# Feed-forward down projections as seven block products in place of eight

## The chip, the cores and the metric

The kernel runs on one core of a Trainium2 chip. What counts is the device time of one execution, in microseconds (us), as the median of several runs. The engines are named as the profile names them: PE is TensorE (matrix products), PEld its weight loads, DVE is VectorE, ACT is ScalarE, POOL is GpSimd and SP is SyncE, which here only issues transfers.

## What the reference computes

A network over 256 tokens of width 1024, in float32 throughout. Its front is two layers of three sublayers; four of these six sublayers are gated feed-forward blocks:

```
def swiglu(h, w_gu, w_down):                     # h: 256 x 1024
    gate, up = jnp.split(h @ w_gu, 2, axis=-1)   # w_gu: 1024 x 5632
    return (jax.nn.silu(gate) * up) @ w_down     # w_down: 2816 x 1024

def sublayer(x, shift, scale, gate, g_pre, g_post, fn, res_weight):
    h = rmsnorm(x, g_pre) * (1 + scale[:, None, :]) + shift[:, None, :]
    return x + res_weight * gate[:, None, :] * rmsnorm(fn(h), g_post)
```

Shift, scale and gate ("modulation") of every sublayer are products of one conditioning row with a large weight matrix, 11 such matrices in all. The other two sublayers are a gated linear attention and a latent attention. The tail is a short convolution, differential attention and two expert layers, each of which gathers 128 rows of 8 KB for each of the 256 tokens from a table.

## The kernel before

**Stages.** The front is eight stages in one fixed order: ffn, gla, ffn, kv, ffn, mla, ffn, conv (numbered 0 to 7, so the feed-forward stages are 0, 2, 4 and 6). The 256 tokens are two blocks of 128, b = 0 and 1. Every engine runs its own written-out list of instructions, with counting semaphores between the lists, and each list is worked off in order.

**First part of a feed-forward stage** (`ffn` on PE, the matmuls of L975). The hidden width 2816 is 22 tiles of 128. For each tile a unit of 16 float32 matmuls of 256 columns makes gate and up in one PSUM bank (three banks `psW` in turn; a unit opens only when the unit three before has been stored). ACT takes the silu, DVE multiplies (L2207) and stores one tile of `actT` (in `arena`), and counts `unit_stored`. The profile records each float32 matmul as two rows.

**Second part** (`project`, L893). 22 tiles of activations times 22 weight tiles of 128 x 1024, for two token blocks and two halves of 512 columns: 88 matmuls of 512 columns that sum into `psF[:, b, :]`. It begins when DVE has stored the last tile. The last 12 matmuls are those of block 1 for tiles 16 to 21, so block 0 is complete 12 matmuls before the end. Then ACT makes block 0's root mean square, DVE adds it to `x` (`finish`) and scales the next stage's input (`prepare`), and PE, behind its last down matmul, transposes that input (L786) for the next stage.

**Weights.** SP loads them into `ring`, four slots of 2 MB each: 11 loads of gate and up, 6 of down (four tiles each, the last two), then the next stage's. A slot is filled again when `w_used` (down) or `unit_full` (gate and up) says that it is free.

**Modulation.** The modulation matrices come as 120 halves of 1 MB. POOL issues their loads into three buffers (`modulation_weights`, L509), each when the one three before was used; DVE multiplies and sums each in two instructions of 1024 elements (`half_step`, L2032). They are spread over the feed-forward stages by `halves_done`: 4/3 of a half for each unit of the first part, and what is left (6 of 32 in stages 0 and 6, 2 of 28 in stages 2 and 4) in the second, by a loop after the last unit. DVE has them in its list between the units' products.

**Kept chunks.** Three 1 MB chunks of tail weights (numbers 3, 6 and 9) are loaded into `arena` by SP between the conv stage's first weight loads.

## Time and profile before

| what | us |
| --- | --- |
| median of 3 runs (2773.39 to 2774.01) | 2773.78 |
| span of the profiled execution | 2775.9 |
| first part of a feed-forward stage, 640 matmul rows | 138.2 to 138.5 |
| down projection of one stage, 176 matmul rows | 75.8 |
| front, up to the first gathered rows of the tail | 1358.7 |
| tail, from there on | 1417 |

The profiled execution's span is 2.1 us above the median of the runs; its own device time is not given apart. The page cuts the span into 40 slices of 69.4 us. The GB/s row is what all transfers of the core moved in a slice. In stretches given as A:B, the figures are the length, then busy time of PE, PEld, DVE, ACT and POOL with their instructions, the granted TensorE clock, the DMA share and GB/s.

### The profile page before, as it was taken

The page shows a single profiled execution, that of the slowest core. Times are in us where ns is not written, and L with a number is a line of the kernel's source. Part 1 is how long each engine was busy: PE and PEld are TensorE (multiplying, and loading weights), DVE is VectorE, ACT ScalarE, POOL GpSimd, SP SyncE. Part 2 cuts the span into 40 slices and gives each one's busy share as a digit, 9 for nine tenths or more (in the row PEclk, how much of TensorE's full clock was granted, in tenths as well). Part 3 has the DMA queues.
Part 4 walks back from the last instruction along what each step waited for, and adds up shares of the span by engine and source line. Part 5 has one row for each costly group of instructions (what it writes and reads, how often), then busy time and mean ns, then how long its engine had stood idle before and what let it go on. Part 6 is the DMA issues. An engine that isn't in the chain of part 4 may idle for free.

```text
span 2775.9 us, 26672 instructions
## 1 busy us (share of the span) xinstructions
PE 2463.2 (89%) x9819; PEld 1566.6 (56%) x9819; DVE 1601.6 (58%) x3550; ACT 620.1 (22%) x1778; POOL 685.0 (25%) x698
## 2 busy tenths in 40 slices
PE   7999999999999999999998877967988778877776
PEld 6874558856884678758654432634535535432222
DVE  4552144524451545513697885686887877874445
ACT  2001210001000220000143333342333533332222
POOL 1110001100110001100243443444444443444332
PEclk9999999999999999999999999989999989999999
DMA  9994427954894339957799999999999999999997
GB/s 382 383 372 165 152 95 271 361 231 152 319 363 170 144 149 380 370 202 269 293 376 421 421 422 421 413 412 421 415 421 400 421 421 415 421 392 422 421 422 326
DMA packets 120520, 931.58 MB, mean 336 GB/s; under 512 B 15133, under 2 KB 16565, under 8 KB 20422
## 3 DMA queue, kind: packets, MB, share of 16 engines
q0 software_dynamic: 94032, 670.65, 59.1%
q1 hardware_dynamic: 26358, 259.23, 23.7%
q8 instruction: 77, 1.26, 0.2%
q14 instruction: 53, 0.43, 0.0%
HBM read 928.74 MB, written 1.09 MB: 335 GB/s over the span
## 4 chain that ended last, share of the span: by engine, by line
PE 58%; DMA 27%; DVE 8%; ACT 3%; issue 2%; SPq 1%; POOL 1%; DVEq 0%
DMA ring<-in_peer_uv_dram,lamt 26%; PE psR L975 20%; PE psF L893 11%; PE psF L1325 10%; DVE ring L2567 3%; PE psR L863 2%; PE psR L833 2%; PE psR L822 2%; PE psR L1350 1%; POOL ring L679 1%; PE psR L1422 1%; PE psF L921 1%; PE psR L874 1%; ACT small L1765 1%; PE psF L1192 1%
## 5 line engine op out<-in xcount | busy, mean ns | idle before, releaser
L1325 PE MATMUL psF<-ring,p_diag 128*128 128x512 f32 x1792 | 868.2, 629 | 248.0 <-ACT p_diag L1771 247.7
L679 POOL DMA_INDIRECT ring<-in_peer_uv_dram,lamt x512 | 592.8, 1158 | 984.3 <-PE psF L1325 757.9
L2567 DVE SCALAR_TENSOR_TENSOR ring<-ring,h 128x1024 f32<-128x1024 f32 x512 | 620.9, 1223 | 345.5 <-DMA ring<-in_peer_uv_dram,lamt 342.4
L1325 PEld LDWEIGHTS psF<-ring,p_diag 128*128 128x128 f32 x1792 | 337.0, 198 | 709.3 <-ACT p_diag L1771 369.4
L975 PE MATMUL psR<-hT,ring 128*128 128x256 f32 x2560 | 553.3, 379 | 0.6 <-DMA ring<-in_gu_t_dram 0.6
L975 PEld LDWEIGHTS psR<-hT,ring 128*128 128x128 f32 x2560 | 486.2, 190 | 66.5 <-DMA ring<-in_gu_t_dram 0.7
L893 PE MATMUL psF<-ring,arena 128*128 128x512 f32 x704 | 303.2, 593 | 4.0 <-DVE arena L2207 4.0
L1762 ACT ACTIVATE small<-small 128x2 f32<-128x2 f32 x255 | 51.8, 203 | 825.6 <-DVE ring L2567 825.4
L893 PEld LDWEIGHTS psF<-ring,arena 128*128 128x128 f32 x704 | 133.5, 190 | 172.0 <-issue 166.4
L509 POOL DMA_DIRECT2D mring<-in_mod_t_dram x80 | 42.5, 531 | 746.3 <-DVE mring L2032 742.2
L2207 DVE TENSOR_TENSOR arena<-arena,psR 128x256 f32<-128x256 f32 x80 | 33.7, 421 | 249.7 <-ACT arena L1632 249.6
L1771 ACT ACTIVATE p_diag<-ident,small 128x128 f32<-128x128 f32 x446 | 158.2, 395 | 8.3
L1632 ACT ACTIVATE arena<-psR 128x256 f32<-128x256 f32 x86 | 33.0, 384 | 568.7 <-PE psR L975 522.7
L1765 ACT ACTIVATE small<-small,gout 128x1 f32<-128x1 f32 x510 | 122.4, 287 | 8.3
L2032 DVE SCALAR_TENSOR_TENSOR mring<-mring,M 128x1024 f32<-128x1024 f32 x96 | 113.6, 1220 | 13.4 <-DMA mring<-in_mod_t_dram 13.3
L2122 DVE RECIPROCAL small<-small 128x1 f32<-128x1 f32 x12 | 1.9, 157 | 201.6 <-ACT small L1616 201.6
L509 POOL DMA_DIRECT2D M<-in_mod_t_dram x40 | 21.2, 530 | 331.3 <-DVE M L2032 301.9
L2549 DVE SCALAR_TENSOR_TENSOR hT<-ring,small,hT 128x1024 f32<-128x1024 f32 x62 | 79.5, 1282 | 26.9 <-ACT small L1765 26.6
L1410 PEld LDWEIGHTS psR<-hT,mring 128*128 128x128 f32 x768 | 89.2, 192 | 9.6 <-issue 9.6
L1410 PE MATMUL psR<-hT,mring 128*128 128x128 f32 x768 | 89.6, 275 | 0.0
L2009 DVE COPY arena<-psR 128x512 f32<-128x512 f32 (+5 forms) x48 | 29.9, 629 | 90.0 <-PE psR L863 53.7
L2032 DVE SCALAR_TENSOR_TENSOR mring<-mring,p_diag 128x1024 f32<-128x1024 f32 x64 | 75.7, 1220 | 10.4 <-DMA mring<-in_mod_t_dram 10.3
(341 smaller groups left out, 2289.3 us busy)
## 6 DMA issues: line engine op xcount, KB each, us to landing
ring<-in_gu_t_dram SPq DMA_DIRECT2D x44, 2048.0 KB, 9.0
mring<-in_mod_t_dram POOLq DMA_DIRECT2D x80, 1024.0 KB, 7.8
M<-in_mod_t_dram POOLq DMA_DIRECT2D x40, 1024.0 KB, 8.1
ring<-in_down_t_dram SPq DMA_DIRECT2D x20, 2048.0 KB, 9.3
mring<-in_tail_w_dram SPq DMA_DIRECT2D x40, 1024.0 KB, 9.3
ring<-in_conv_in_t_dram SPq DMA_DIRECT2D x12, 2048.0 KB, 8.1
ring<-in_gla_in_t_dram SPq DMA_DIRECT2D x6, 2048.0 KB, 7.7
ring<-in_out_t_dram SPq DMA_DIRECT2D x6, 2048.0 KB, 7.7
```

Of the source, the lines that this page charges most:

```text
L509: eng.dma_start(half_rows[i % HALVES].rearrange("p k n -> p (k n)"), w).then_inc(m_loaded[i % HALVES], 16)
L679: pool.indirect_dma_start(out=pair(n % PAIRS), out_offset=None, in_=rows, in_offset=bass.IndirectOffsetOnAxis(ap=s_idx[:, c:c + 1], axis=0 ...
L822: ins = pe.matmul(ps[:, t * P:(t + 1) * P], w[:, k, t * P:(t + 1) * P], hT[:, k, b * P:(b + 1) * P], start=(k == 0), stop=(k == KD - 1))
L893: ins = pe.matmul(psF[:, b, f * HALF:(f + 1) * HALF], lhs[:, k, b * P:(b + 1) * P], w[:, k % 4, f * HALF:(f + 1) * HALF], start=(k == 0), ...
L975: ins = pe.matmul(ps[:, part * T:(part + 1) * T], w[:, k, part * 256 + c * P:part * 256 + (c + 1) * P], hT[:, k, :], start=(k == 0), stop= ...
L1325: ins = pe.matmul(psF[:, b, f * HALF:(f + 1) * HALF], p_diag[:, n % PAIRS, :], row_v(n % PAIRS)[:, f * HALF:(f + 1) * HALF], start=(i == 0 ...
L1410: ins = pe.matmul(ps[:, t * P:(t + 1) * P], w[:, k, t * P:(t + 1) * P], hT[:, k, b * P:(b + 1) * P], start=(k == 0), stop=(k == KD - 1))
L1765: act.activation(p_w[:, c + s:c + s + 1], p_gel[:, c + s:c + s + 1], ACT.Copy, scale=s_g[:, b, i + s:i + s + 1]).then_inc(w_ready, 1)
L1771: act.activation(p_diag[:, c + s, :], ident[:], ACT.Copy, scale=p_w[:, c + s:c + s + 1])\
L2032: ins = dve.scalar_tensor_tensor(w[:, t, :], w[:, t, :], 1.0, cond_row[st.n >= 7], ALU.mult, ALU.mult, accum_out=dst[:, t:t + 1])
L2549: ins = dve.scalar_tensor_tensor(sums, row, p_w[:, c:c + 1], sums, ALU.mult, ALU.add)
L2567: dve.scalar_tensor_tensor(row_u(c), row_u(c), 1.0, h[:, b, :], ALU.mult, ALU.mult, accum_out=p_dots[:, c:c + 1]).then_inc(dot_done, 1)
```

## The change

The 22 tiles of the hidden width are taken as 11 pairs (k, kk) = (2p, 2p + 1). For each pair, with token blocks A (two tiles by two blocks) and weight halves B (two tiles by two halves of 512), the eight block products become seven, and the results are combined by adds after the sums over the pairs are complete.

- PE: `project` for down is replaced by `down`: 77 matmuls of 512 columns into seven banks. Pairs 0 to 4 run all seven products; pairs 5 to 8 run products 1, 6, 7, 5, 4; then the last two pairs run these five product by product; then come products 2 and 3 of pairs 5 to 10 (12 matmuls). It begins one unit's store earlier (`have(u - 2)`).
- POOL: `sum_weights` makes for each pair four differences of 128 x 512 in SBUF, two of them linked by a wait each. There are two buffers, in the place of `h` (even pairs) and `hT` (odd pairs). Pair 0 runs four halves before the stage's last half is issued; pair 1 waits until the first part has no unit left; pairs 2 to 10 wait until product 4 of the pair two before is done. All are ahead of the next stage's modulation loads in POOL's list.
- DVE: `sum_acts` makes four sums of 128 x 128 for each pair, between the units' products. `sum_products` and `sum_second` combine the seven banks into `psF` (eight instructions of 512 columns), and ACT waits for `down_summed` in place of the matmuls.
- Modulation: `halves_done` spreads all of a stage's halves over the units up to tile 21, 1.6 a unit in stages 0 and 6 and 1.4 in stages 2 and 4. None is left for the second part.
- Loads: the down tiles are stored in the order 0 to 9, then 10, 12, ... 20, then 11, 13, ... 21. Kept chunk 6 now comes first, and chunks 3 and 9, whose homes hold sums of activations, wait for the end of stage 6.

```diff
-PRELOADED = (3, 6, 9)
+PRELOADED = (6, 3, 9)
+PAIRED = FT // 2
+LATE_PAIRS = range(5, PAIRED)
+DOWN_ORDER = [k for p in range(5) for k in (2 * p, 2 * p + 1)] + [2 * p for p in LATE_PAIRS] + [2 * p + 1 for p in LATE_PAIRS]
+ACT_SUMS = (7552, 10752, 10752, 8704)
...
+    def act_sum(which, m, p):
+        q = m * PAIRED + p
+        return arena[:, ACT_SUMS[which] + q * P:][:, 0:P] if q < 30 else macc[:, 0, (q - 30) * P:(q - 29) * P]
+    def down_tile(st, k):
+        q = DOWN_ORDER.index(k)
+        return slot(st.w + 11 + q // 4, 4, D)[:, q % 4, :]
+    def product_bank(st, product):
+        if product in (6, 7):
+            return psW[(st.u + 17 + product) % 3]
+        return {1: psM[:], 4: psF[:, 0, 0:HALF], 5: psF[:, 0, HALF:], 2: psF[:, 1, 0:HALF], 3: psF[:, 1, HALF:]}[product]
...
-        return min(2 * len(BESIDE[st.n]), max(unit - 1, 0) * 4 // 3)
+        return min(2 * len(BESIDE[st.n]), max(unit - 1, 0) * 2 * len(BESIDE[st.n]) // 20)
...
-            if c in PRELOADED:
+            if c == PRELOADED[0]:
                 sp.wait_ge(x_ready, x_count(6))
+            elif c in PRELOADED:
+                sp.wait_ge(w_used, outputs[ffn3.w + LOADS["ffn"] - 1])
...
-                if st is conv7 and j in (2, 3, 4):
-                    load_kept(PRELOADED[j - 2])
+                if st is conv7 and j in (2, 4, 5):
+                    load_kept(PRELOADED[(2, 4, 5).index(j)])
...
+        def sum_weights(st, p):
+            k, kk = 2 * p, 2 * p + 1
+            w, ww = down_tile(st, k), down_tile(st, kk)
+            if p >= 2:
+                pool.wait_ge(weights_sums_used, (PAIRED - 2) * st.which + p - 1)
+            for i in sorted({down_slot(k), down_slot(kk)}):
+                pool.wait_ge(w_loaded[home_of(st.w + 11 + i)], landed[st.w + 11 + i])
+            if p == 1:
+                pool.wait_ge(unit_full, st.u + UNITS["ffn"])
+            if p == 0:
+                pool.wait_ge(unit_stored, st.u + 6)
+            t2, t3, t4 = [weight_sums[p % 2][:, m, :] for m in range(3)]
+            b11, b12, b21, b22 = w[:, 0:HALF], w[:, HALF:], ww[:, 0:HALF], ww[:, HALF:]
+            pool.tensor_tensor(t3, b22, b12, ALU.subtract)
+            link(pool.tensor_tensor(b12, b12, b11, ALU.subtract))
+            link(pool.tensor_tensor(t2, b22, b12, ALU.subtract))
+            pool.tensor_tensor(t4, b21, t2, ALU.subtract).then_inc(weights_summed, 1)
...
+                    for before, p in ((4, range(0, 1)), (0, range(1, PAIRED))):
+                        for st in stages:
+                            if st.kind == "ffn" and i == 2 + sum(2 * len(BESIDE[k]) for k in BESIDE if k <= st.n) - before:
+                                for q in p:
+                                    sum_weights(st, q)
+            if n == len(PIECES):
+                for p in range(1, PAIRED):
+                    sum_weights(ffn3, p)
...
-        def project(st, i, lhs, kt):
...
+        def down(st):
+            def product(m, p):
+                k, kk = 2 * p, 2 * p + 1
+                w, ww, sums = down_tile(st, k), down_tile(st, kk), weight_sums[p % 2]
+                lhs, rhs = {1: (actT[:, k, P:], w[:, 0:HALF]), 2: (actT[:, kk, P:], ww[:, 0:HALF]),
+                            3: (act_sum(st.which, 2, p), ww[:, HALF:]), 4: (actT[:, kk, 0:P], sums[:, 2, :]),
+                            5: (act_sum(st.which, 0, p), w[:, HALF:]), 6: (act_sum(st.which, 1, p), sums[:, 0, :]),
+                            7: (actT[:, k, 0:P], sums[:, 1, :])}[m]
+                return pe.matmul(product_bank(st, m), lhs, rhs, start=(p == 0), stop=(p == PAIRED - 1))
+            def sums_ready(p):
+                pe.wait_ge(act_summed, PAIRED * st.which + p + 1)
+                pe.wait_ge(weights_summed, PAIRED * st.which + p + 1)
+            for p in range(PAIRED - 2):
+                sums_ready(p)
+                for m in (1, 6, 7, 5):
+                    ins = product(m, p)
+                if p == 6:
+                    ins.then_inc(w_used, 1)
+                product(4, p).then_inc(weights_sums_used, 1)
+                if p not in LATE_PAIRS:
+                    for m in (2, 3):
+                        ins = product(m, p)
+                    if p in (1, 3):
+                        ins.then_inc(w_used, 1)
+            for m in (1, 6, 7, 5, 4):
+                for p in (PAIRED - 2, PAIRED - 1):
+                    if m == 1:
+                        sums_ready(p)
+                    ins = product(m, p)
+                    if m == 4 and p == PAIRED - 2:
+                        ins.then_inc(w_used, 1)
+                ins.then_inc(first_ready if m == 4 else product_done, 1)
+            for m in (2, 3):
+                for p in LATE_PAIRS:
+                    ins = product(m, p)
+                    if m == 3 and p == 8:
+                        ins.then_inc(w_used, 1)
+                ins.then_inc(product_done if m == 2 else w_used, 1)
...
-            have(u - 1)
-            project(st, st.w + 11, actT, FT)
+            have(u - 2)
+            down(st)
...
-                    output_done(act, st, b)
+                    if st.kind == "ffn":
+                        act.wait_ge(down_summed, TB * st.which + b + 1)
+                    else:
+                        output_done(act, st, b)
...
+                if j % 2 == 0:
+                    dve.wait_ge(unit_stored, u - 1)
+                    sum_acts(st, j // 2 - 1)
-            while halves_taken.n < sum(2 * len(BESIDE[n]) for n in BESIDE if n <= st.n):
-                half_step()
+            dve.wait_ge(unit_stored, u)
+            sum_acts(st, PAIRED - 1)
+            if st.n == 0:
+                tables()
+            sum_products(st)
+        def sum_acts(st, p):
+            k, kk = 2 * p, 2 * p + 1
+            b0, b1 = [[actT[:, t, b * P:(b + 1) * P] for t in (k, kk)] for b in range(TB)]
+            s1, s2, s4 = [act_sum(st.which, m, p) for m in range(3)]
+            link(dve.tensor_tensor(s1, b0[0], b0[1], ALU.add))
+            dve.tensor_tensor(b0[0], b1[0], b0[0], ALU.subtract)
+            link(dve.tensor_tensor(s2, s1, b1[0], ALU.subtract))
+            dve.tensor_tensor(s4, b1[1], s2, ALU.subtract).then_inc(act_summed, 1)
+        def sum_products(st):
+            done = 5 * st.which
+            dve.wait_ge(product_done, done + 1)
+            dve.tensor_copy(sum_p1, product_bank(st, 1)).then_inc(product_summed, 1)
+            dve.wait_ge(product_done, done + 2)
+            dve.wait_ge(product_summed, 4 * st.which + 1)
+            dve.tensor_tensor(sum_p16, product_bank(st, 6), sum_p1, ALU.add).then_inc(product_summed, 1)
+            dve.wait_ge(product_done, done + 3)
+            dve.wait_ge(product_summed, 4 * st.which + 2)
+            dve.tensor_tensor(sum_p167, product_bank(st, 7), sum_p16, ALU.add).then_inc(product_summed, 1)
+            dve.wait_ge(product_done, done + 4)
+            ps = product_bank(st, 5)
+            dve.tensor_tensor(sum_p165, ps, sum_p16, ALU.add).then_inc(product_summed, 1)
+            dve.wait_ge(product_summed, 4 * st.which + 4)
+            dve.tensor_tensor(ps, ps, sum_p167, ALU.add)
+            dve.wait_ge(first_ready, sum(s.kind != "kv" for s in stages[:st.n + 1]))
+            ps = product_bank(st, 4)
+            dve.tensor_tensor(ps, ps, sum_p167, ALU.add).then_inc(down_summed, 1)
+        def sum_second(st, half):
+            if half == 0:
+                dve.wait_ge(product_done, 5 * st.which + 5)
+                ps = product_bank(st, 2)
+                dve.tensor_tensor(ps, ps, sum_p1, ALU.add)
+            else:
+                output_done(dve, st, 1)
+                ps = product_bank(st, 3)
+                dve.tensor_tensor(ps, ps, sum_p165, ALU.add).then_inc(down_summed, 1)
...
-            if st.n == 0:
-                tables()
                     finish(st, b)
+                if st.kind == "ffn" and b == 0:
+                    sum_second(st, 0)
                 if b or st.kind not in ("kv", "mla"):
                     prepare(every[st.n + 1], b)
+                if st.kind == "ffn" and b == 0:
+                    sum_second(st, 1)
...
-    given["down_t"] = np.stack([tile(w) for w in inputs["ffn_w_down"].reshape(4, FF, D)])
+    given["down_t"] = np.stack([tile(w.reshape(FT, P, D)[DOWN_ORDER].reshape(FF, D)) for w in inputs["ffn_w_down"].reshape(4, FF, D)])
```

## Rows read from the trace of the kernel before

**Rows 1.** The page: its head, and granted clock and GB/s by slice

```profile
span 2775.9 us, 26672 instructions
...
PEclk9999999999999999999999999989999989999999
...
GB/s 382 383 372 165 152 95 271 361 231 152 319 363 170 144 149 380 370 202 269 293 376 421 421 422 421 413 412 421 415 421 400 421 421 415 421 392 422 421 422 326
```

**Rows 2.** Chain of waits, start to first mixer: start us, us, what

```profile
48.09 138.41 PE psR L975 x640
187.49 75.80 PE psF L893 x176
```

**Rows 3.** Stretches of the span: its us, busy time by engine, clock, DMA share, GB/s

```profile
48.00:186.50 138.50, 138.40 (x640) 121.56 (x640) 73.20 (x163) 7.30 (x19) 18.31 (x35) 1.00 0.96 385
187.00:263.30 76.30, 75.81 (x178) 33.68 (x179) 25.42 (x61) 5.93 (x10) 3.70 (x7) 1.00 0.54 209
...
1018.60:1156.80 138.20, 138.16 (x641) 121.30 (x639) 71.07 (x152) 7.67 (x21) 21.89 (x42) 1.00 0.91 353
...
1233.60:1300.00 66.40, 65.11 (x496) 57.48 (x495) 20.94 (x60) 1.40 (x3) 0.00 (x0) 1.00 0.85 339
...
1358.70:2775.00 1416.30, 1143.25 (x3935) 602.55 (x3933) 1020.46 (x2230) 479.28 (x1473) 586.93 (x507) 0.96 0.99 411
```

**Rows 4.** Groups by line and shape, whole span

```profile
L893 PE MATMUL psF<-ring,arena 128*128 128x512 f32 x704 | 303.2, 593 | 4.0 <-DVE arena L2207 4.0
...
L2516 DVE TENSOR_TENSOR macc<-gains,small 128x512 f32<-128x512 f32 x32 | 22.2, 694 | 1.1
...
L2448 DVE SCALAR_TENSOR_TENSOR arena<-arena 128x128 f32<-128x128 f32 x32 | 9.1, 346 | 0.3
```

**Rows 5.** Timeline where the down projection of stage 2 begins

```profile
570.68 0.42 DVE L2207 TENSOR_TENSOR arena<-arena,psR 128x256 f32<-128x256 f32 x1 [4.00 <-ACT arena L1632]
...
571.15 15.29 PE L893 MATMUL psF<-ring,arena 128*128 128x512 f32 x35 [1.00 <-DVE arena L2207]
...
573.68 0.53 POOL L509 DMA_DIRECT2D M<-in_mod_t_dram  x1 [6.38 <-DVE M L2032]
```

**Rows 6.** Timeline of GpSimd's own arithmetic: start us, us

```profile
5.30 0.40 POOL L709 CAST dist<-dist 128x256 f32<-128x256 int32 x1
5.85 0.40 POOL L710 TENSOR_SCALAR_AFFINE_SELECT dist<-dist 128x256 f32<-128x256 f32 x1 [0.15 <-POOL dist L709]
...
6.53 0.20 POOL L713 CAST small<-small 128x16 f32<-128x16 int32 x1
```

**Rows 7.** Stretches of the tail: two idle gaps, each with what follows

```profile
1818.30:1823.00 4.70, 0.03 (x2) 0.00 (x0) 2.29 (x7) 2.70 (x9) 1.56 (x2) 1.00 1.00 415
1823.50:1826.90 3.40, 3.40 (x7) 1.58 (x6) 3.38 (x6) 0.03 (x1) 0.09 (x1) 0.50 1.02 424
1896.80:1902.30 5.50, 0.02 (x1) 0.00 (x0) 3.64 (x7) 1.64 (x5) 2.69 (x2) 0.97 1.01 422
1902.00:1905.40 3.40, 3.08 (x4) 1.17 (x4) 3.36 (x4) 0.27 (x1) 0.00 (x0) 0.50 1.02 424
```

**Rows 8.** Timeline of VectorE near the end of stage 0's first part

```profile
173.54 1.22 DVE L2032 SCALAR_TENSOR_TENSOR mring<-mring,M 128x1024 f32<-128x1024 f32 x1
...
176.22 1.23 DVE L2032 SCALAR_TENSOR_TENSOR mring<-mring,M 128x1024 f32<-128x1024 f32 x1
```

**Rows 9.** Who waited for whom, first part of stage 0

```profile
DVE mring L2032 <- DMA mring<-in_mod_t_dram: 8.4, 4, 3.5
```

**Rows 10.** Timeline, end of stage 0's down projection

```profile
253.02 1.02 ACT L1615 ACTIVATE h<-psF 128x1024 f32<-128x1024 f32 x1 [36.97 <-PE psF L893]
...
260.36 0.75 DVE L2110 TENSOR_SCALAR h<-x,small 128x1024 f32<-128x1024 f32 x1
...
263.12 1.04 PE L786 MATMUL psR<-ident,h 128*128 128x128 f32 x8
...
263.84 2.65 DVE L2086 TENSOR_SCALAR hT<-psR,small 128x128 f32<-128x128 f32 x8 [2.72 <-PE psR L786]
```

More of the change, by code:

```diff
@@ L314, in _program @@
     m_reduced = sem("m_reduced")
+    act_summed = sem("act_summed")
+    weights_summed = sem("weights_summed")
+    weights_sums_used = sem("weights_sums_used")
+    product_done = sem("product_done")
+    product_summed = sem("product_summed")
+    down_summed = sem("down_summed")
     unit_full = sem("unit_full")
```

27 lines of the change are left out of this document (6 added, 21 removed).

## The prediction

> **What bounds the kernel now.** I read the slices of the page first. From slice 21 to the end the transfers run at 400 to 422 GB/s in nearly every slice [rows 1]; that is the tail, and as one stretch it is at a DMA share of 0.99 [rows 3]. The change touches nothing in it, so the tail should only move as a block: what the front gains or loses is the result. In the front I read the chain of waits. The first feed-forward stage stands in it with two long pieces and nothing beside them: 138.41 us of gate and up matmuls, then 75.80 us of down matmuls [rows 2]. Stages 2, 4 and 6 repeat them within 0.3 us. So PE sets the time there, and a PE microsecond saved or lost in a feed-forward stage counts in full, four times over. The stretches show what lies beside it: in the first part of stage 0, PE is busy 138.40 of 138.50 us and the transfers are at a share of 0.96, 385 GB/s; in the second part DVE, ACT and POOL are nearly free and the transfers at 209 GB/s [rows 3]. The granted clock is 1.00, the 2.4 GHz level, in these stretches.
>
> **The terms on PE.** One float32 matmul of 512 columns takes 75.80 / 88 = 0.861 us (two recorded rows each) [rows 2, 4]. Eleven fewer are 9.5 us. The second part also begins sooner: at its start PE waits 1.00 us for DVE's product of the last tile [rows 5], 4.0 us over the four stages [rows 4]; `have(u - 2)` asks for the tile before, long stored. Together 10.5 us a stage, 42 us in all. That is the most the change can give.
>
> **What GpSimd takes back.** The sums of weights are new on POOL, and PE waits for them at the head of each pair. No two-input arithmetic of GpSimd is in this trace. Its one-input operations take 0.40 us for 256 columns and 0.20 us for 16 [rows 6], so 0.20 + 0.20 x 496/240 = 0.61 us for 512. Lower bound of a two-input difference of 512 columns: the same 0.61 us. Upper bound: two such passes, 1.22 us. I take 1.2 us, near the upper end, because this engine's rows grow with each element that it reads, and the second operand is a second reading. A linked operation starts 0.15 us after the one before [rows 6]; with two links a pair costs G = 4 x 1.2 + 0.3 = 5.1 us. By the bounds G is 2.7 to 5.2 us.
>
> The Trainium skill's page "GPSIMD Engine Reference", section "Performance versus the Vector engine", gives 4497 ns for a `tensor_tensor` add of 2048 float32 columns, about twice VectorE's, and advises against such work on GpSimd. A quarter of it is 1.12 us, an estimate from that page: G would be 4.8 us and the change some 5 us better than my sum. No run here shows it yet.
>
> Now the schedule, from PE's start of the part at 0. Pairs 0 to 4 take 7 x 0.861 = 6.03 us each, pairs 5 to 10 have only five products ahead, 4.31 us each. Pair 0's sums are made during the first part. Pair 1's need `hT`, free at 0, and are there at 0.2 + 5.1 = 5.3, before 6.03: no wait, with 0.7 us in hand. Pairs 2 to 6 have room. From then on PE's step is 4.31 us and POOL's is 5.1. POOL can start pair 7 when product 4 of pair 5 is done, at 5 x 6.03 + 4.31 = 34.5, and wakes 0.2 to 0.3 us later (POOL's issue at 573.68 after DVE's work that ended at 573.4) [rows 5]. It then makes pairs 7, 8, 9 and 10 without pause, so pair 10 is ready at 34.7 + 4 x 5.1 + 0.1 = 55.2. PE would want it at 30.15 + 4 x 4.31 + 0.86 = 48.2, because the last two pairs run product by product and pair 10 is wanted after a single matmul of pair 9. PE loses 7.0 us: about 1.1 + 0.8 + 0.8 at pairs 7 to 9 and 4.3 at pair 10. Even fast sums leave a part: POOL may start pair 10 only when PE starts pair 9, so the wait is at least G + 0.3 - 0.86, 2.1 us at G = 2.7.
>
> **What the clock takes back.** In the tail PE idled for 4.70 and 5.50 us in two stretches at 1.00 and 0.97, and in the 3.4 us that followed the granted clock was 0.50, the 1.2 GHz level, in both [rows 7]. The 4.3 us before pair 10 is such a gap. At half clock 3.4 us do the work of 1.7: I add 1.7 us a stage. Bounds: 0 if the clock stays, 3.4 if the low level lasts twice as long.
>
> **DVE and the boundary.** Combining costs eight instructions of 512 columns, 0.69 us each by the nearest row [rows 4]. Six lie under PE's last products; on block 0's way lies one, after product 4. Before, block 0's input for the next stage was ready at 260.36 + 0.75 = 261.1, and PE came to it at 263.12 [rows 10]: 2.0 us in hand, and the add takes 0.8. `sum_second(0)` falls into DVE's wait for ACT's root. `sum_second(1)` stands ahead of the storing of the transposed input: it starts when PE ends, about 263.3, takes 0.69, and the storing starts near 264.05, in place of 263.84. I count 0.2 us a stage. ACT's square of block 1 comes 0.7 us later, but its root then waited for DVE anyway. If the 2.0 us in hand were gone, the add would cost 0.8 us a stage.
>
> **The first part.** Sums of activations: 44 instructions of 128 columns a stage, 0.35 us each by the nearest row [rows 4], 1.4 us in every second unit. A half of modulation takes 2.7 us of DVE (173.54 to 176.22) [rows 8]. In stage 0 a unit then asks of DVE 1.6 x 2.7 + 0.42 + 0.7 = 5.4 us of its 6.9. It fits, and PE meets a late DVE only when it is about two units (13.8 us) behind, or one unit at the start of the second part. The transfers are the tighter side: 385 GB/s for 138.5 us are 53.3 MB; some three more halves of 1.05 MB must land inside, 408 GB/s, against the 422 that the tail holds [rows 1, 3]. DVE waited 8.4 us in four waits for modulation there even at the old pace [rows 9], so it will lag at first. I put 1 us on stage 0, bounds 0 and 8, and nothing on stage 6 (353 becomes some 376 GB/s) [rows 3] or on the others, with 28 halves. If the sums of pair 0 come late they have the last two units as cover: their slot is free seven units before the part ends.
>
> **Loads.** In the second part there are no modulation halves any more; the 2 MB of down slot 4 are asked for when pair 1 is done, at 12, and wanted by POOL at 22.6 for pair 5, which has 2.4 us of its own in hand: covered. In conv, chunks 3 and 9 land up to 17 us after stage 6, where 339 GB/s flow over 66 us [rows 3]; 1 MB more is 2.5 us of transfers, and each 2 MB weight load is asked for a slot or more ahead of its use. I cost both at nothing; without that cover the chunks would cost 2.5 us each.
>
> **Sum.** A stage: -9.5 - 1.0 + 7.0 + 1.7 + 0.2 = -1.6 us. Four stages: -6.3; with stage 0's 1: -5.3. On the profiled execution, 2775.9 becomes 2770.6; the median of the runs stands 2.1 us under that span, so 2773.8 becomes 2768.5, -0.19%, just inside the 0.2% (5.5 us) that I take as what a measurement of this kernel can tell from no change.
>
> **The rivals.**
> (a) My forecast, POOL's pace of 4.8 to 5.4 us gives nearly all back: -11 to +1 us. Chance 0.43.
> (b) The sums are quick, G at most 4.3, as the one-input rows alone would have it: PE then waits 2.0 to 3.9 us a stage. With the clock's fall at 4.3, -4 x 4.7 + 1 = -18; without it at 2.7, -4 x 8.2 + 1 = -32. About 2750. Chance 0.2. For it: the short rows [rows 6]; against: they read one operand.
> (c) The clock does not fall after the wait, or POOL overlaps its instructions so that G is near 4.6: -12, 2762. Chance 0.1.
> (d) Slower: GpSimd's sums in the down part cost more than two one-input passes. At G = 5.5 the stage is even; above 5.8 POOL is behind in the seven-product pairs too, and each 0.1 us of G costs about 0.9 us a stage. At G = 6.0 PE waits 12 us, a stage loses 3.5, in all +15: 2789. For it: no row bounds a two-input operation from above by measurement, and both operands are in the memory that transfers fill meanwhile. Chance 0.17.
> (e) Stage 0, or 0 and 6, become bound by transfers in the first part, because all halves and all gate and up weights now want 408 GB/s: PE waits some 8 us, 2776. For it: the share of 0.96 and the waits [rows 3, 9]; against: 408 is still 3% under what the tail holds. Chance 0.1.
>
> Faster by over 0.2%: half of (a) less a little, all of (b) and (c): 0.48. Within 0.2%: the rest of (a) and (e)'s greater part: 0.28. Slower: (d) and part of (e): 0.24. The range leaves out the far half of (b) and of (d): 2750 to 2786. The forecast's own range is 2762 to 2775.
>
> **What would show it.** In the profile of the changed kernel: 154 down rows of PE a stage; GpSimd's differences near 1.2 us, a pair every 5.1 us from pair 6 on; PE's waits for POOL, 28 us in all, the longest 4 us just before pair 10; a granted clock of 0.5 for some 3 us behind it; no wait for DVE at the start of the part; the part, from start to last matmul, near 75 us; first parts of 138.2 us, stage 0's up to 1 more; the tail as long as before. I am wrong if a pair of sums takes under 4.5 or over 5.5 us, if PE waits in a first part, or if the next stage starts late.

## The result: 0.7% slower, and the profile after

Median of 4 runs after the change: 2794.81 us (2793.65 to 2795.81); of 4 runs of the kernel before beside them: 2773.90 (2773.39 to 2778.68). The ratio is 1.007 (95% interval 1.0055 to 1.0084): 20.9 us slower, where 5.3 us faster was forecast, and outside the range, which ended at 2786. The profiled execution after has a span of 2791.9 us in 2793.65 us of its own. The one before has a span of 2775.9 us, and its tail was the longer by 4.4 us (1433.1 against 1428.7 us), though the change touches nothing there; so the fronts are compared and not the spans. The first gather of rows is issued at 1342.8 us before (a mark earlier than the 1358.7 of the table of times) and at 1363.2 after: these 20.4 us, nearly the whole result, lie in the front.

Cut at marks that both traces have (a down part runs from the last gate and up matmul to PE's first transpose of the next stage's input; the rest of the front is what lies between stage 0's first gate and up matmul and the first gather, less the four first parts and the four down parts):

| us | stage 0 | stage 2 | stage 4 | stage 6 | sum | rest of the front |
| --- | --- | --- | --- | --- | --- | --- |
| before | 76.6 | 76.6 | 76.6 | 76.6 | 306.5 | 434.9 |
| after | 84.5 | 79.1 | 78.2 | 85.3 | 327.1 | 435.1 |
| forecast for it | 75.0 | 75.0 | 75.0 | 75.0 | 300.2 | 434.9 |
| after: of this at clock 0.50 | 13.7 | 6.8 | 6.8 | 13.7 | 41.0 | |

The rest of the front holds what follows a boundary and moved by 0.2 us; the first parts stay at 138.3, stage 0's too, where the forecast had placed its 1 us. The loss is in the four down parts: 7.9 and 8.7 us in stages 0 and 6, 2.4 and 1.5 in stages 2 and 4. In stretches (length, busy PE, PEld, DVE, ACT, POOL, clock, DMA share, GB/s), first part of stage 0, the four down parts, and two short pieces of the first, the profile after has

```profile
47.90:186.20 138.30, 138.26 (x642) 121.37 (x640) 92.48 (x211) 7.67 (x21) 24.59 (x41) 1.00 0.98 399
186.20:270.70 84.50, 71.99 (x155) 30.64 (x156) 44.37 (x65) 6.31 (x11) 58.10 (x45) 0.92 0.42 161
577.70:656.70 79.00, 70.44 (x154) 29.84 (x153) 22.13 (x28) 4.52 (x8) 55.42 (x43) 0.96 0.37 138
844.50:922.60 78.10, 69.41 (x154) 29.32 (x154) 20.98 (x27) 4.52 (x8) 55.45 (x43) 0.96 0.38 140
1168.40:1253.70 85.30, 71.97 (x154) 30.64 (x155) 30.24 (x45) 3.07 (x5) 56.64 (x42) 0.92 0.44 167
246.00:250.40 4.40, 0.41 (x1) 0.00 (x0) 0.00 (x0) 0.00 (x0) 4.24 (x5) 0.72 0.00 0
250.50:254.00 3.50, 3.50 (x5) 1.44 (x6) 0.69 (x1) 0.00 (x0) 1.35 (x3) 0.50 0.64 211
```

The 154 down rows of PE are there, against 176 [rows 2], and PE's busy time fell from 75.8 us to between 69.4 and 72.0, although it holds half-clock matmuls. A part of 78 to 85 us with 69 to 72 busy has 9 to 13 us of waits. POOL, nearly idle there before, works 55 to 58 us. The last two rows are the wait before stage 0's pair 10 and what follows it: a clock of 0.50, the 1.2 GHz level. Who waits for whom on PE, stages 2 (first fence) and 6 (second); the figures are us in total, times, and the longest:

```profile
PE psR L959 <- POOL h L746: 4.6, 2, 4.0
PE psR L959 <- POOL hT L746: 3.9, 3, 2.2
```

```profile
PE psR L959 <- POOL hT L746: 6.9, 3, 5.2
PE psR L959 <- POOL h L746: 4.6, 2, 4.0
...
PE psR L959 <- DVE arena L2288: 1.8, 1, 1.8
```

`h` holds the even pairs: the 4.6 are 0.6 at pair 8 and 4.0 at pair 10, near the forecast's 0.8 and 4.3. The `hT` waits hold the surprise: 2.2 and 5.2 us before pair 1, where I had none. The two blockers, POOL and VectorE, in the timeline around it in stage 2:

```profile
577.82 1.26 POOL L743 TENSOR_TENSOR hT<-ring 128x512 f32<-128x512 f32 x1 [7.22 <-PE psR L1053]
578.19 0.42 DVE L2288 TENSOR_TENSOR arena<-arena,psR 128x256 f32<-128x256 f32 x1 [2.95 <-ACT arena L1710]
...
579.05 2.24 POOL L744 TENSOR_TENSOR ring<-ring 128x512 f32<-128x512 f32 x1
...
580.10 2.27 DVE L2113 SCALAR_TENSOR_TENSOR mring<-mring,p_diag 128x1024 f32<-128x1024 f32 x1
581.37 2.13 POOL L745 TENSOR_TENSOR hT<-ring 128x512 f32<-128x512 f32 x1
...
582.41 1.10 DVE L2117 TENSOR_TENSOR small<-small,brow 128x2 f32<-128x2 f32 x1
583.43 1.21 DVE L2113 SCALAR_TENSOR_TENSOR mring<-mring,p_diag 128x1024 f32<-128x1024 f32 x1
583.57 2.19 POOL L746 TENSOR_TENSOR hT<-ring,hT 128x512 f32<-128x512 f32 x1
...
585.91 2.05 PE L959 MATMUL psR<-ring,arena 128*128 128x512 f32 x2 [2.24 <-POOL hT L746]
```

Three of POOL's four differences take 2.1 to 2.2 us in place of 1.26, and beside them a multiply of VectorE takes 2.27 in place of 1.22 and an add of two columns 1.10 in place of 0.16. VectorE is still at the modulation halves of the last unit, and the two engines seem to take turns: its add of two columns ends at 583.51, POOL's difference at 583.50. But VectorE's product of an SBUF and a PSUM operand (L2288) is at its usual 0.42, and POOL's difference beside it at 1.26. PE's matmul behind the wait takes 2.05 for 1.02: half clock again. In stage 4 PE has the same wait of 2.2 us before pair 1, and the clock stays up. What follows the wait in stage 2 and in stage 4:

```profile
586.00:589.40 3.40, 3.40 (x5) 1.42 (x6) 3.26 (x6) 0.00 (x0) 3.32 (x3) 0.52 0.00 0
852.80:856.20 3.40, 3.40 (x8) 1.52 (x9) 3.33 (x5) 0.00 (x0) 3.33 (x2) 1.00 0.00 0
```

Later in stage 0, with VectorE idle, POOL keeps its own pace:

```profile
238.78 1.26 POOL L746 TENSOR_TENSOR h<-ring,h 128x512 f32<-128x512 f32 x1
240.00 1.26 POOL L743 TENSOR_TENSOR hT<-ring 128x512 f32<-128x512 f32 x1
241.22 1.27 POOL L744 TENSOR_TENSOR ring<-ring 128x512 f32<-128x512 f32 x1
242.57 1.26 POOL L745 TENSOR_TENSOR hT<-ring 128x512 f32<-128x512 f32 x1
243.91 1.26 POOL L746 TENSOR_TENSOR hT<-ring,hT 128x512 f32<-128x512 f32 x1
```

A pair every 5.13 us (forecast 5.1). At the start of stage 0's down part POOL comes to pair 1 late, behind its last load issue, which waits for VectorE:

```profile
191.26 0.53 POOL L543 DMA_DIRECT2D mring<-in_mod_t_dram  x1 [3.35 <-DVE mring L2113]
191.80 1.81 POOL L743 TENSOR_TENSOR hT<-ring 128x512 f32<-128x512 f32 x1
193.59 2.23 POOL L744 TENSOR_TENSOR ring<-ring 128x512 f32<-128x512 f32 x1
```

and VectorE is late because of transfers, by the waits in the first part of stage 0:

```profile
DVE M L2113 <- DMA M<-in_mod_t_dram: 27.6, 10, 4.6
...
DVE mring L2113 <- DMA mring<-in_mod_t_dram: 4.7, 3, 1.7
```

That is 32.3 us at 399 GB/s and a share of 0.98, where before it was 8.4 [rows 9] and 1.7 for `M`, 10.1 in all, at 385. The forecast had 408 GB/s for the same stretch.

### The profile page after: what moved, and what is told of

The parts are those of the page before. It is cut to its first block and busy times, and to the rows that moved or that the text cites. A ratio compares the mean times of both kernels' runs of the same rounds, so it can differ in the third digit from the quotient of the medians.

```text
span 2791.9 us, 26974 instructions
## 1 busy us (share of the span) xinstructions
PE 2445.7 (88%) x9731; PEld 1555.2 (56%) x9731; DVE 1723.4 (62%) x3758; ACT 620.0 (22%) x1778; POOL 921.3 (33%) x874
## 3 DMA queue, kind: packets, MB, share of 16 engines
q8 instruction: 77, 1.26, 0.2%
## 5 line engine op out<-in xcount | busy, mean ns | idle before, releaser
L715 POOL DMA_INDIRECT ring<-in_peer_uv_dram,lamt x512 | 586.4, 1145 | 945.0 <-PE psF L1403 759.5
L2113 DVE SCALAR_TENSOR_TENSOR mring<-mring,M 128x1024 f32<-128x1024 f32 x96 | 119.4, 1280 | 5.3 <-DMA mring<-in_mod_t_dram 5.3
L959 PE MATMUL psF<-ring,arena 128*128 128x512 f32 x240 | 113.4, 592 | 0.0
L2288 DVE TENSOR_TENSOR arena<-arena,psR 128x256 f32<-128x256 f32 x80 | 33.6, 421 | 121.3 <-ACT arena L1710 121.2
L2113 DVE SCALAR_TENSOR_TENSOR mring<-mring,p_diag 128x1024 f32<-128x1024 f32 x64 | 82.7, 1328 | 22.9 <-DMA mring<-in_mod_t_dram 22.9
L959 PE MATMUL psR<-ring,arena 128*128 128x512 f32 x88 | 53.2, 690 | 43.1 <-POOL hT L746 21.2
```

The source lines that it names most:

```text
L715: pool.indirect_dma_start(out=pair(n % PAIRS), out_offset=None, in_=rows, in_offset=bass.IndirectOffsetOnAxis(ap=s_idx[:, c:c + 1], axis=0 ...
L959: return pe.matmul(product_bank(st, m), lhs, rhs, start=(p == 0), stop=(p == PAIRED - 1))
L2113: ins = dve.scalar_tensor_tensor(w[:, t, :], w[:, t, :], 1.0, cond_row[st.n >= 7], ALU.mult, ALU.mult, accum_out=dst[:, t:t + 1])
```

## The experiments

The theory after this: the weight sums' pace costs what the forecast said, and two things were missed, the collision of VectorE's multiplies with POOL's differences, and the late modulation of stages 0 and 6. The rivals: the extra is all lateness; or it is all the clock. "Part" is the length of a down part as in the table above. e1, e3, e5b and e9 leave work out, and each was run once: their times have no interval, and the argument goes by the parts in their profiles.

**e1: the multiplies made short.** The loads and issues stay.

```diff
-                ins = dve.scalar_tensor_tensor(w[:, t, :], w[:, t, :], 1.0, cond_row[st.n >= 7], ALU.mult, ALU.mult,
+                ins = dve.scalar_tensor_tensor(w[:, t, 0:64], w[:, t, 0:64], 1.0, cond_row[st.n >= 7][:, 0:64], ALU.mult, ALU.mult,
```

> The changed kernel with each modulation multiply cut from 1024 to 64 columns (the rest of each modulation sum is left out); every transfer stays. In the changed kernel PE waited for pair 1's weight sums 4.7, 2.2, 2.2 and 5.2 us in stages 0, 2, 4, 6, and single GpSimd differences took 2.24 us in place of 1.26 while VectorE ran its multiplies. Theory A (VectorE and GpSimd instructions that both have two operands in SBUF exclude each other): all GpSimd differences of pair 1 take 1.26 us, pair 1 costs 5.1 us and its wait is gone in stages 2 and 4; in stages 0 and 6 it goes too if VectorE's lateness made POOL issue its last half late. Theory B (the differences are slow at the start because the transfers fill the same memory, or because hT is freed late): pair 1 keeps its 7.9 us in stages 2 and 4 and the wait stays 2.2 us. The wait of 1.5 and 1.8 us at the start of stages 0 and 6 should go if it comes from VectorE being behind, and stay if the transfers alone make it. Sum by theory A: waits of 14.3 us and the start waits of 3.3 us go, with 3 to 7 us of low clock behind them: about 2774.

Measured: 2767.86 us (before, beside it, 2776.22). Parts 75.8, 75.6, 75.3, 75.2, 0.2 to 0.8 above the forecast's 75.0: without the two things missed its sum nearly holds. (Each part has the clock at 0.50 for 6.8 us here, the length of my upper bound; 1.5 to 2.8 of them fall in the wait itself.) VectorE still waits for modulation transfers in stage 0's first part, 69.9 us in all (40.7 and 29.2), but with multiplies this short it is never late for PE. So the late transfers cost PE something only together with multiplies of full length. This experiment takes away both things at once, so the others part them.

**e2: the new pace of modulation alone, in the kernel before.**

```diff
-        return min(2 * len(BESIDE[st.n]), max(unit - 1, 0) * 4 // 3)
+        return min(2 * len(BESIDE[st.n]), max(unit - 1, 0) * 2 * len(BESIDE[st.n]) // 20)
```

> The kernel before with one part of the change alone: all modulation halves in the first part of each feed-forward stage (1.6 or 1.4 a unit in place of 4/3). My theory: VectorE falls behind in stages 0 and 6 for want of transfers (it waited 32 and 33 us for them in the changed kernel, 10 us before) but PE sees it only at the start of the down projection, 1 to 9 us in stages 0 and 6 where the last tile's product is waited for (have(u - 1)), and not in stages 2 and 4: 2774 to 2792, likeliest 2785. Rival: VectorE catches up when no activation sums and no GpSimd differences compete, so PE's wait stays 1.0 us a stage and the time is that of before, 2774.

Measured: 2788.54 us (before, beside it, 2776.22), ratio 1.0046 (1.0029 to 1.0063). Parts 83.4, 76.6, 76.6, 80.4: 10.6 us, all in stages 0 and 6. In stage 0 PE waits at the start of the part for VectorE's product, then has the low clock:

```profile
PE psF L893 <- DVE arena L2207: 5.3, 1, 5.3
```

```profile
191.50:195.00 3.50, 3.25 (x4) 1.51 (x5) 1.27 (x2) 0.00 (x0) 0.29 (x1) 0.50 1.00 428
```

VectorE waited 41.2 us for modulation transfers in stage 0's first part (before: about 10). The pace costs 10.6 us with no block product and no arithmetic of GpSimd in play.

**e3: the weight sums made short** (16 columns of 512).

```diff
-            t2, t3, t4 = [weight_sums[p % 2][:, m, :] for m in range(3)]
-            b11, b12, b21, b22 = w[:, 0:HALF], w[:, HALF:], ww[:, 0:HALF], ww[:, HALF:]
+            t2, t3, t4 = [weight_sums[p % 2][:, m, 0:16] for m in range(3)]
+            b11, b12, b21, b22 = w[:, 0:16], w[:, HALF:HALF + 16], ww[:, 0:16], ww[:, HALF:HALF + 16]
```

> The changed kernel with GpSimd's differences cut from 512 to 16 columns (the rest of each weight difference is left out), about 0.2 us each. It shows what seven products give when their sums cost nothing. If the waits for GpSimd (39.5 us in all) and the low clock behind them are the whole loss: down parts of 66.3 us plus a start wait of 0 to 1.8 us in stages 0 and 6, nine to ten us less than before in each stage, so 2774 - 40 + 3 = 2737. If PE loses something else in the new order (more weight switching, a later next stage), the parts stay above 67 us.

Measured: 2740.69 us. Parts 68.4, 66.5, 66.5, 68.5; clock 1.00 throughout:

```profile
563.60:630.10 66.50, 66.14 (x155) 28.97 (x154) 15.04 (x28) 4.52 (x8) 12.02 (x43) 1.00 0.44 163
```

Before's 76.6 less the 10.5 of the forecast is 66.1, and the 0.4 above it are a last wait of PE before pair 10. So the whole gain on PE is real, and nearly everything given back hangs on the duration of POOL's differences. That holds for the greater part of the lateness too: short sums catch up.

**e4: PE kept awake before pair 10**, by 15 small products into an idle bank.

```diff
+                        if p == PAIRED - 1:
+                            pe.wait_ge(unit_stored, st.u + UNITS["ffn"])
+                            for _ in range(15):
+                                pe.matmul(psW[(st.u + 25) % 3][:, 0:P], ident[:], ident[:], start=True, stop=True)
                         sums_ready(p)
```

> The changed kernel with 15 dummy matmuls of 128 columns (about 3.7 us at full clock) into a free bank ahead of the wait for pair 10's sums; nothing is left out. In the changed kernel PE idled 4.0 us there and the granted clock was at half for 3.4 to 6.8 us behind it in all four stages. If the idle time causes the fall: no low clock behind pair 10, 1.7 to 3.4 us less in each stage, 7 to 14 us in all, 2781 to 2788. If the fall comes from the shorter waits before pairs 7 to 9 or from something else, it stays and the time is 2794.

Measured: 2788.34 us, ratio 1.0041 (1.0027 to 1.0055), against 1.007. Parts 83.9, 77.4, 76.1, 82.4, 7.3 us less than after (0.6, 1.7, 2.1 and 2.9). The stretches that answer to the last two of after:

```profile
246.00:250.50 4.50, 3.90 (x28) 3.24 (x28) 0.00 (x0) 0.00 (x0) 4.38 (x4) 1.00 0.00 0
250.50:254.00 3.50, 2.81 (x12) 1.62 (x12) 0.69 (x1) 0.00 (x0) 2.82 (x4) 1.00 0.32 44
```

The clock stays at 1.00 there. The low clock behind pair 10 costs 7.3 us, on average 1.8 a stage (forecast 1.7), and the median of the runs is 6.5 us under that of the changed kernel, a third of the loss. That is not the rival that it is all the clock; but the low clock behind pair 1's wait in stages 0, 2 and 6 is still there in this run.

**e5b: short loads in the fast stream.** The modulation loads keep their number and waits but, from the sixth on, bring 256 columns of 2048; VectorE multiplies as long as before, by zero.

```diff
+        n = 256 if i >= 5 else 2048
-        eng.dma_start(half_rows[i % HALVES].rearrange("p k n -> p (k n)"), w).then_inc(m_loaded[i % HALVES], 16)
+        eng.dma_start(half_rows[i % HALVES].rearrange("p k n -> p (k n)")[:, 0:n], w[:, 0:n]).then_inc(m_loaded[i % HALVES], 16)
...
-                ins = dve.scalar_tensor_tensor(w[:, t, :], w[:, t, :], 1.0, cond_row[st.n >= 7], ALU.mult, ALU.mult,
+                ins = dve.scalar_tensor_tensor(w[:, t, :], w[:, t, :], 0.0, cond_row[st.n >= 7], ALU.mult, ALU.mult,
```

> The changed kernel with the modulation loads from the sixth on cut from 1 MB to 128 KB; VectorE's multiplies keep their 1024 columns but multiply by zero, so the modulation sums are left out (only the biases remain). Theory: in stages 0 and 6 the want of transfers makes VectorE late, and with it POOL's last issue and so pair 1's differences; in all four stages pair 1 also meets VectorE's last multiplies. So with short loads the start waits (1.5 and 1.8 us) go, and the waits for pair 1 in stages 0 and 6 fall from 4.7 and 5.2 to the 2.2 us of stages 2 and 4, with one low clock less: stages 0 and 6 some 6 to 7 us shorter each, stages 2 and 4 as in the changed kernel. In all about 2782. Rival: the memory is busy with transfers and that slows GpSimd: then pair 1 takes 5.1 us in all stages and its wait is gone everywhere, about 2776.

Measured: 2779.38 us (before 2775.28). Parts 77.4, 79.1, 78.2, 78.4: stages 0 and 6 lose their extra (7.2 and 7.0 us), stages 2 and 4 don't move. PE's waits in stage 0's down part:

```profile
PE psR L960 <- POOL h L747: 5.4, 3, 4.0
PE psR L960 <- POOL hT L747: 2.9, 3, 1.2
```

The wait of 4.7 us before pair 1 is down to about 1.2, and the one for VectorE's product is gone. So lateness is 14.1 us, it goes when the transfers are short, and in stages 2 and 4 there is none.

**e6: product 1 ahead of the wait for the sums**, which it doesn't use.

```diff
+            def first_product(p):
+                arrived(st.w + 11 + down_slot(2 * p))
+                return product(1, p)
...
+                first_product(p)
                 sums_ready(p)
-                for m in (1, 6, 7, 5):
+                for m in (6, 7, 5):
...
-                    if m == 1:
+                    if m == 6:
                         sums_ready(p)
-                    ins = product(m, p)
+                    ins = first_product(p) if m == 1 else product(m, p)
```

> The changed kernel with the wait for a pair's weight sums moved behind product 1, which reads no sums; in the last passage both pairs' product 1 and pair 9's product 6 go ahead of the wait for pair 10. If the order alone sets the 4.0 us wait before pair 10, it becomes 4.0 - 1.7 = 2.3 us, the waits before pair 1 fall by 0.86 us where there are any, and those before pairs 7 to 9 (POOL's pace) stay 2.3 us in sum, as POOL starts each later pair no sooner. A stage 2.6 us shorter, and less low clock: 2774 to 2785, likeliest 2780. Rival: POOL's pace rules the whole passage, so a wait left out at one place comes back at another: 2790 or more.

Measured: 2786.98 us, ratio 1.0038 (1.0024 to 1.0053). Parts 82.0, 75.0, 75.1, 82.7. I had expected the wait before pair 10 to fall to 2.3 us. It did not; stage 2 again:

```profile
PE psR L959 <- POOL h L746: 4.6, 2, 4.0
PE psR L959 <- POOL hT L746: 1.6, 2, 1.4
```

Yet the four parts are 12.3 us shorter than after (2.5, 4.1, 3.1 and 2.6), about the 2.6 us a stage that the expectation named. Pair 10 is ready three of POOL's 5.13 us behind pair 7, in both kernels. What changed is how far PE is by then: it has two more products behind it when it waits for pair 10, so less is left to do, and from the end of that wait to the transposes it is 18.0 us in stage 2 against 19.8 after. The waits in that stage came to 6.2 us in place of 8.6: before pair 1 1.4 for 2.2, and none before pair 9. The low clock behind pair 1's wait is gone there too. The time shows less of this than the parts, 7.8 us between the two medians, and in this profile the rest of the front is 438.5 us, 3.4 longer than after: the clock was at 0.50 for 3.4 us more in each of two stretches between the stages, which the edit does not touch, and each of them is 1.7 us longer.

**e9: the multiplies replaced by plain sums** (one SBUF operand each).

```diff
-                ins = dve.scalar_tensor_tensor(w[:, t, :], w[:, t, :], 1.0, cond_row[st.n >= 7], ALU.mult, ALU.mult,
-                                               accum_out=dst[:, t:t + 1])
+                ins = dve.tensor_reduce(dst[:, t:t + 1], w[:, t, :], AX, ALU.add)
```

> The changed kernel with VectorE's modulation multiply (two operands in SBUF, 1.22 us) replaced by a plain sum of the same 1024 columns (one operand in SBUF, about 1.1 us); the multiplication with the conditioning row is left out. In the changed kernel a GpSimd difference took 2.24 us where it met a multiply, and VectorE's add of 128x2 took 1.10 in place of 0.16. Theory A (they exclude each other only where both have two operands in SBUF, or one of them holds both read paths): the differences of pair 1 fall to 1.26 us beside the plain sums, and rise only beside the few two-operand adds; the wait before pair 1 falls from 2.2 us to 0 to 0.8 in stages 2 and 4. Rival (any reading of SBUF by VectorE slows GpSimd): the differences stay near 2.2 us and the wait stays 2.2. Stages 0 and 6 stay late for want of transfers. In all 2783 to 2790 by theory A, 2794 by the rival.

Measured: 2782.72 us (before 2776.64). Parts 81.5, 74.9, 74.9, 82.6. The same place in stage 2, POOL and VectorE:

```profile
575.67 2.34 DVE L2113 TENSOR_REDUCE small<-mring 128x1 f32<-128x1024 f32 x2
576.20 1.26 POOL L744 TENSOR_TENSOR ring<-ring 128x512 f32<-128x512 f32 x1
577.54 1.27 POOL L745 TENSOR_TENSOR hT<-ring 128x512 f32<-128x512 f32 x1
578.04 0.78 DVE L2116 TENSOR_TENSOR small<-small,brow 128x2 f32<-128x2 f32 x1
578.75 2.33 DVE L2113 TENSOR_REDUCE small<-mring 128x1 f32<-128x1024 f32 x2
578.88 1.27 POOL L746 TENSOR_TENSOR hT<-ring,hT 128x512 f32<-128x512 f32 x1
...
581.69 1.07 DVE L2305 TENSOR_TENSOR arena<-arena 128x128 f32<-128x128 f32 x1
```

VectorE works there as long as before (two sums in 2.34, 1.17 each), yet pair 1's differences take 1.26 to 1.27 us, and the wait before pair 1 is gone in stages 2 and 4. What collides is the kind of operands, not the time of work: VectorE's two-operand adds of 128 columns beside them still stretch, 1.07 for 0.28. The plain sum also leaves out the multiply's output of 1024 columns, which e9 alone can't tell from the second operand; but the product with one PSUM operand, which writes 256 columns to SBUF, ran beside a difference with neither of them longer (0.42 and 1.26), and an add that writes two columns was held up. Stages 0 and 6 keep their lateness, as they should; stage 6's first part is 2.0 us longer here.

The Trainium skill says this: on its page "SBUF — State Buffer", section "Who interferes with whom", a VectorE instruction with two SBUF inputs and a GpSimd instruction that reads SBUF hold a shared port exclusively in turns, while one SBUF input, or a plain reduction, does not contend. The traces agree in each of the three (2.24 for 1.26; the PSUM product at 0.42; the plain sum at 1.17).

**e7: the weight sums moved to VectorE**, nearly idle in the down part; modulation back at its old pace, its left-over halves one by one between pairs.

```diff
+            for p in range(1, PAIRED):
+                if p > 1:
+                    sum_weights(st, p)
+                if st.n == 0 and p == 5:
+                    tables()
+                elif p in (1, 2, 3, 4, 6, 8) or (st.n and p == 5):
+                    if halves_taken.n < sum(2 * len(BESIDE[n]) for n in BESIDE if n <= st.n):
+                        half_step()
...
+            dve.tensor_tensor(t3, b22, b12, ALU.subtract)
+            link(dve.tensor_tensor(b12, b12, b11, ALU.subtract))
+            link(dve.tensor_tensor(t2, b22, b12, ALU.subtract))
+            dve.tensor_tensor(t4, b21, t2, ALU.subtract).then_inc(weights_summed, 1)
```

Pair 0 follows tile 20's product, pair 1 stands ahead of the last tile's.

> Seven products as in the changed kernel, but the weight sums by VectorE (4 x 0.69 us a pair by its own rows), which is idle in the down part, and the modulation halves at their old pace of 4/3 a unit, the rest between VectorE's sums. By my account the loss is made of GpSimd's pace (5.13 us a pair against PE's 4.31), pair 1's collision, the moved modulation and the low clock behind the waits. Then only the wait before pair 10 is left, 2.9 + 0.1 - 0.86 = 2.1 us, and perhaps one low clock: down parts of 66.5 + 2.1 + 0 to 3.4 us in place of 76.6, 8 to 4 us less in each stage: 2742 to 2758, likeliest 2745. Rival: VectorE's list is too full beside PE (its halves wait for transfers and hold the sums up), and stages 0 and 6 keep 3 to 8 us of waits: 2755 to 2765.

Measured: 2747.14 us, ratio 0.9896 (0.988 to 0.9913). Parts 71.6, 68.5, 68.5, 68.5. VectorE's sums of a pair in its timeline:

```profile
195.09 0.69 DVE L2294 TENSOR_TENSOR h<-ring 128x512 f32<-128x512 f32 x1
195.71 0.68 DVE L2295 TENSOR_TENSOR ring<-ring 128x512 f32<-128x512 f32 x1
196.42 0.69 DVE L2296 TENSOR_TENSOR h<-ring 128x512 f32<-128x512 f32 x1
197.15 0.69 DVE L2297 TENSOR_TENSOR h<-ring,h 128x512 f32<-128x512 f32 x1
```

That is 2.75 us a pair, [rows 4]'s 0.69 each. PE's only wait for sums in stage 2 is 2.1 us before pair 10, the forecast's floor of 2.1 for G = 2.7, and no low clock follows it. In stage 0 PE waits 2.6 us more at pairs 6 and 7, where `tables()` stands between VectorE's sums.

**e8: e7 with the wait moved as in e6.** The same edit.

> The kernel with VectorE's sums and the later wait together. The wait before pair 10 should be 2.9 + 0.1 - 2.6 = 0.4 us and no low clock in the down parts: 67.0 us each in place of 76.6, 38 us less in all, 2736. If the clock falls anyway or the next stage waits for block 0 (whose way has VectorE's sums ahead of it), 2740 to 2748.

Measured: 2739.65 us, ratio 0.9869 (0.9853 to 0.9886). Parts 69.1, 66.5, 66.5, 66.5. Here the wait before pair 10 itself falls, from 2.1 to 0.4, and the parts are 8.6 us shorter than in e7.

**e10: e8 with stage 0's `tables()` behind the sums** and halves after pairs 1 to 6.

```diff
-                if st.n == 0 and p == 5:
-                    tables()
-                elif p in (1, 2, 3, 4, 6, 8) or (st.n and p == 5):
+                if p in (1, 2, 3, 4, 5, 6):
...
+            if st.n == 0:
+                tables()
             sum_products(st)
```

> VectorE's sums with the later wait, and stage 0's rotary tables (5.6 us of VectorE's list, 1.9 of it a wait for ACT) moved from between pairs 5 and 6 to behind pair 10; the halves that were behind pairs 6 and 8 now stand behind 5 and 6. In the run without this PE lost 2.4 us in stage 0 at pairs 6 and 7 (69.06 us against 66.52 in the other stages). If the tables were the cause, stage 0's part becomes 66.5 to 67.5 and the time 2 us less, 2737.5. If the tables behind pair 10 delay block 0's sums instead, PE waits at the next stage's start and nothing is won: 2739.7.

Measured: 2736.67 us (2733.85 to 2737.02), ratio 0.9851 (0.9837 to 0.9864), 40 us under the kernel before. It has the lowest median here, but its interval overlaps with e8's. What the edit gives is 1.0 us of stage 0's part, where I had expected 1.6 to 2.6. Parts 68.1, 66.5, 66.5, 66.5:

```profile
186.40:254.40 68.00, 66.31 (x154) 28.80 (x153) 57.12 (x116) 6.32 (x11) 4.24 (x8) 1.00 0.65 241
559.70:626.20 66.50, 66.14 (x155) 29.01 (x154) 43.89 (x76) 4.52 (x8) 2.12 (x4) 1.00 0.47 179
```

**e11: e7 with the new pace of modulation.** The edit of e2.

> VectorE's weight sums with the changed kernel's modulation pace (all halves in the first part). The pace alone cost the kernel before 6.8 us in stage 0 and 3.8 in stage 6 and nothing in stages 2 and 4. VectorE is 5 to 9 us behind at the end of these first parts and now also owes pair 1's sums there, so PE should wait about 4 to 9 us at the start or before pair 1 in stages 0 and 6, with a low clock behind it: 2747 + 6 to 14, likeliest 2757. If GpSimd's share was the whole trouble, the time stays 2747.

Measured: 2765.48 us, ratio 0.996 (0.9947 to 0.9974). Parts 79.9, 68.9, 68.5, 78.8. The pace costs 18 us, all but 0.4 of it in stages 0 and 6, more than the 6 to 14 that I expected: with the sums on VectorE, a late VectorE delays the sums too. PE's waits in stage 6's down part:

```profile
PE psR L932 <- DVE h L2297: 9.5, 3, 4.6
...
PE psR L932 <- DVE hT L2297: 0.9, 1, 0.9
```

## Why the prediction was wrong

Reading the four parts from the full gain downwards, as sums of parts: all gains and nothing given back would be 306.5 - 42 = 264.5 (e10 is at 267.7). POOL's pace with the clock behind pair 10 brings it to 301.9 (e1), the collision to 313.0 (e5b), the lateness to 327.1 (after). These terms act on one another. The lateness is the difference of e5b and after, but with short sums (e3) it costs 4 us and not 14. The collision is a difference of two experiments: 8.9 of its 11.1 us are longer waits of PE, the rest is clock. In stages 2 and 4 it is 6.4 us; there e9, one edit from after, gives 7.4.

**What held.** The matmul's 0.861 us, eleven fewer, and the start: 66.5 us with quick sums. G = 5.1: 5.13. "PE loses 7.0 us" at pairs 7 to 10: in stage 0 1.11 + 0.60 + 0.60 + 4.03 = 6.3. The clock's 1.7 a stage: 1.8 by e4 on average, between 0.6 and 2.9. Chunks and down loads at nothing: the rest of the front moved by 0.2 us. Together 9.4 us a stage given back (301.9 less 264.5, by four) against the forecast's 8.9. Part of this nearness is luck: in e1 the waits for POOL are 6.3 us a stage, 0.7 under the forecast, and the other 3.0 us stand against 1.9 for clock and boundary. The clock is at 0.50 for 4.0 to 5.3 us of PE's work in each of e1's parts, which is 2.0 to 2.7 us lost by the forecast's own reckoning. The boundary's 0.2 was 0.09: VectorE begins to store the transposed input 0.81 us behind the first transpose after, 0.72 before.

**The step that failed first: "pair 1's ... are there at 0.2 + 5.1 = 5.3, before 6.03: no wait, with 0.7 us in hand".** The sum was made with VectorE idle. But VectorE is then still at the last unit's halves, and each of its multiplies reads two SBUF operands: POOL's four differences took 7.9 us in place of 5.1, and PE waited 2.2 us in stages 2 and 4. In stage 2 a half-clock stretch of 3.4 us came behind this wait, in stage 4 none did, but there the low clock behind pair 10 lasted 6.8 us, against stage 2's 3.4. The collision came to 11.1 us in all. The trace of before could have told when VectorE works, but not what that does to POOL, since no POOL arithmetic ran beside it. I had read the Trainium skill's figure for the pace and not weighed its rule on the port.

**The other: "I put 1 us on stage 0, bounds 0 and 8, and nothing on stage 6".** The reckoning was in bandwidth: 408 GB/s are under the 422 that the tail holds. But by the program each modulation load is issued only when the buffer three before is free, so a load that takes longer to land makes the next one late. VectorE waited 32 us in stage 0 and 33 (22.9 + 10.1) in stage 6, for 10 and none before. Its last product came late (PE's start waits of 1.5 and 1.8), POOL's last issue came 5.1 and 5.7 us after the end of the first part, and behind it in POOL's list stand the sums. Stage 6 was not safe at "353 becomes some 376": it has the same 32 halves, 1.6 a unit. The transfers ran at 366 GB/s and a share of 0.93 there, so bandwidth was left; but the modulation halves took a median of 9.9 to 10.5 us from issue to landing, against 7.7 to 8.3 before. That this and the three buffers make the lateness is argued from the program; what the runs show is that it goes with short transfers (e5b) or with short multiplies (e1). Alone the pace costs 10.6 us (e2), in this kernel 14.1. Rival (e) had the mechanism but priced it at 8 us and without the queue behind it; (d) came nearest in time, 2789, but for another reason: G is 5.13 but where VectorE's multiplies lie beside the sums, and its doubt was of the transfers.

**Left open.** Why the low clock lasts 3.4 us behind some waits and 6.8 behind others, and why the same wait of 2.2 us is followed by it in stage 2 and not in stage 4, was not tried. Of the remaining 1.6 us of e10's stage 0, 1.4 are PE's wait for the next stage's input, which VectorE makes behind `tables()`; a better place for these was not tried. That the two engines exclude each other by a port is the Trainium skill's account; the runs show the operands on which it depends, not the port.

## What to carry to other kernels

Cost work put on GpSimd with what VectorE does in the same microseconds and how many SBUF operands that reads; a pair of engines can take turns where each alone has time. When a stream of loads is made denser, ask not only whether the bandwidth is enough but what is queued behind the last load's issue, on the issuing engine too. And where a step is bound by one engine's pace, as pair 10 here, look at the length of the stretch and not at the wait alone: moving the wait left the last wait at 4.0 us and still took 12.3 us off the parts. Moving the work to an idle faster engine (0.69 against 1.26 us a difference) gave most: with modulation at its old pace and the later wait as well (e10), the parts were 39 us shorter than before, of the 42 that the change could give.

## Unexpected of the hardware

- An add of two columns on VectorE took 1.10 us in place of 0.16 beside GpSimd's differences and ended with the one beside it. A difference took up to 2.25 us in place of 1.26, a multiply 2.27 in place of 1.22. It isn't always one turn each: late in stage 0's first part an add of 128 columns took 3.05 us in place of 0.28, while GpSimd did two differences at 1.28.
- After a wait of PE of 2.24 us before pair 1 the next matmuls ran at half clock in stage 2 and at full clock in stage 4; after 2.1 us in e7 they ran at full clock.
- At a DMA share of 0.98 in stage 0's first part, 399 GB/s instead of 385, VectorE's waits for modulation rose from about 10 to 32 us.
